# Norm steps and weight splits around five norms: their order on VectorE, ScalarE, GpSimd and TensorE

## The reference, cut to what matters

```python
def rms_norm(x, g):
    xf = x.astype(jnp.float32)
    y = xf * lax.rsqrt(jnp.mean(xf * xf, axis=-1, keepdims=True) + EPS)
    return (y * g.astype(jnp.float32)).astype(x.dtype)

def layer_norm(x, g, b):
    mu = xf.mean(-1, keepdims=True)
    var = jnp.square(xf - mu).mean(-1, keepdims=True)
    return ((xf - mu) * lax.rsqrt(var + LN_EPS) * g + b).astype(x.dtype)
...
        x = x + merged @ w_out[l]
        h2 = rms_norm(x, norm2[l])
        x = x + jnp.square(jax.nn.relu(h2 @ w_up[l])) @ w_down[l]
    return rms_norm(x, final_norm)
...
        x = layer_norm(DN_ALPHA * x + h, ln_g[i, 0], ln_b[i, 0])
        x = layer_norm(DN_ALPHA * x + swiglu_ffn(x, ffn_w_gate_up[i], ffn_w_down[i]), ln_g[i, 1], ln_b[i, 1])
```

## Time and profile before

| | |
|---|---|
| device time, median of 3 runs | 2143.26 us (2142.16 to 2143.68) |
| span of the profiled execution, first to last instruction | 2140.8 us, 2.5 below the median of the runs |
| TensorE, matmuls | busy 2097.3 us, 98% of the span |
| VectorE | busy 1180.6 us, 55% |
| ScalarE | busy 899.8 us, 42% |
| GpSimd | busy 504.1 us, 24% |
| granted TensorE clock, mean | 0.997 |

### The profile page before, as it was taken

The page is one execution under the profiler, slowest core; times in us unless marked ns, Lnnn a source line. Parts: engine busy times, 40 slices in busy tenths (PEclk is TensorE's granted clock), DMA queues, the critical chain, the costliest instruction groups (busy, mean ns, idle before and its releaser), DMA issues. The chain is left out here.

```text
span 2140.8 us, 34365 instructions
## 1 busy us (share of the span) xinstructions
PE 2097.3 (98%) x13883; PEld 1757.1 (82%) x13883; DVE 1180.6 (55%) x2031; ACT 899.8 (42%) x1574; POOL 504.1 (24%) x488
## 2 busy tenths in 40 slices
PE   8999999999999999999999999999999999999998
PEld 7877678988888897867878899899876678899887
DVE  5244546454343455557667678485555646576335
ACT  5454562333232335235444245243566634344231
POOL 4000000100000010211337456382432118363000
PEclk9999999999999999999999999999999999999999
DMA  5312233233333323210023323334342113334321
GB/s 170 98 50 69 60 88 100 70 109 99 98 95 92 99 83 87 79 32 2 3 63 85 112 82 100 99 99 118 79 100 65 51 51 93 94 95 143 99 89 60
DMA packets 341530, 179.64 MB, mean 84 GB/s; under 512 B 44342, under 2 KB 332260, under 8 KB 341372
## 3 DMA queue, kind: packets, MB, share of 16 engines
q1 hardware_dynamic: 339052, 171.54, 28.6%
q0 software_dynamic: 2320, 5.89, 1.0%
HBM read 172.40 MB, written 2.11 MB: 82 GB/s over the span
## 5 line engine op out<-in xcount | busy, mean ns | idle before, releaser
L602 PE MATMUL bank<-act_hi,w_hi 128*128 128x512 f32 (+1 forms) x1568 | 580.5, 370 | 9.5 <-DVE act_lo L1375 2.4
L585 DVE TENSOR_TENSOR w_lo<-w,w_hi 128x1024 fp32r<-128x1024 f32 (+2 forms) x314 | 406.0, 1295 | 317.7 <-ACT w_hi L577 317.3
L604 PE MATMUL bank<-act_hi,w_lo 128*128 128x512 f32 (+1 forms) x1568 | 560.7, 358 | 0.0
L603 PE MATMUL bank<-act_lo,w_hi 128*128 128x512 f32 (+1 forms) x1568 | 560.2, 357 | 0.0
L577 ACT ACTIVATE w_hi<-w 128x1024 fp32r<-128x1024 f32 (+2 forms) x315 | 316.6, 1013 | 294.1 <-PE bank L604 258.8
L602 PEld LDWEIGHTS bank<-act_hi,w_hi 128*128 128x128 f32 x1568 | 296.5, 189 | 63.6 <-issue 16.6
L604 PEld LDWEIGHTS bank<-act_hi,w_lo 128*128 128x128 f32 x1568 | 296.3, 189 | 44.4
L603 PEld LDWEIGHTS bank<-act_lo,w_hi 128*128 128x128 f32 x1568 | 297.0, 189 | 38.0 <-issue 0.7
L602 PE MATMUL bank<-hid_hi,w_hi 128*128 128x512 f32 (+1 forms) x672 | 248.5, 370 | 0.0
L604 PE MATMUL bank<-hid_hi,w_lo 128*128 128x512 f32 (+1 forms) x672 | 247.9, 369 | 0.0
L603 PE MATMUL bank<-hid_lo,w_hi 128*128 128x512 f32 (+1 forms) x672 | 247.9, 369 | 0.0
(11 more groups left out here) (543 smaller groups left out, 3537.3 us busy)
## 6 DMA issues: line engine op xcount, KB each, us to landing
w<-in_ffn_w_gate_up SPq DMA_DIRECT2D x76, 512.0 KB, 3.9
w<-in_w_in SPq DMA_DIRECT2D x41, 512.0 KB, 3.9
w<-in_w_up SPq DMA_DIRECT2D x32, 512.0 KB, 4.1
w<-in_w_down SPq DMA_DIRECT2D x32, 512.0 KB, 3.8
w<-in_ffn_w_down SPq DMA_DIRECT2D x32, 512.0 KB, 4.1
w<-in_even_w_in SPq DMA_DIRECT2D x28, 512.0 KB, 3.8
w<-in_ffn_w_down SPq DMA_DIRECT2D x16, 384.0 KB, 3.5
seven_w<-in_ffn_w_gate_up SPq DMA_DIRECT2D x24, 256.0 KB, 3.2
```

Source lines behind the costliest of these rows:

```text
L585: last = e.tensor_tensor(w_lo[:, at], src, w_hi[:, at].bitcast(F32), ALU.subtract)
L602: e.matmul(s.acc, *first, start=(k == 0), stop=False)
L603: e.matmul(s.acc, *second, start=False, stop=False)
L604: last = e.matmul(s.acc, *third, start=False, stop=(k == kt - 1))
```

## The change

Four things change, in the order of the title. `norms_first` names steps after which a norm's hooks come ahead of the weight split on ScalarE and VectorE, instead of behind it: T5 and T6 at the RMS edges, T6 at the LayerNorm edges. The first half's scaling of an RMS norm moves from T6 (tiles 0 to 3) and T7 (tiles 4 to 7) to T5 and T6. The first spread of a LayerNorm stands at the start of T7 (`a + 4.0`) instead of a quarter into it (`a + 4.25`). The low part of the last tile, `k` = 7, is made by VectorE instead of GpSimd in both halves of all five norms (`pool_lows`). What is computed stays the same.

```diff
         self.late = range(0)
...
@@ Gemm.run, scalar (and the same for vector)
                 s.job.epilogue.scalar(e, self, s)
+                if s.n in self.norms_first:
+                    for hook in hooks:
+                        hook.scalar_after(e, s.n)
                 for part in self.freed_at_once(s.n):
                     self.split_high(e, part)
-                for hook in hooks:
-                    hook.scalar_after(e, s.n)
+                if s.n not in self.norms_first:
+                    for hook in hooks:
+                        hook.scalar_after(e, s.n)
...
@@ Norm.__init__
-        split, odd = high is not None, n // 2
...
+        split = high is not None
+        self.pool_lows = tuple(range(1, min(n, KD - 1), 2))
+        self.dve_lows = tuple(k for k in range(n) if k not in self.pool_lows)
...
@@ Norm.vector_after
-                        if k >= first + 2 and k % 2 == 0 and self.high is not None:
+                        if k >= first + 2 and k - 2 in self.dve_lows and self.high is not None:
                             self.part_low(e, h, k - 2, self.lo)
...
@@ Norm.gpsimd
-            for k in range(1, self.n if self.high is not None else 0, 2):
+            for k in self.pool_lows if self.high is not None else ():
                 self.part_low(e, h, k, self.lo_pool)
...
@@ LayerNorm.gpsimd
-                for n, k in enumerate((1, 3, 5, 7, 0, 2, 4, 6)):
+                for n, k in enumerate(self.pool_lows + self.dve_lows):
...
@@ rms_between
+    g.norms_first |= {b - 2, b - 1}
     return Norm(core, lambda k: core.x[:, k, :], KD, squares, level=(a, b), root=(a + 2.75, head + 3.25),
-                scale=([(b - 1, 0, 4), (b, 4, KD)], b), **kinds)
+                scale=([(b - 2, 0, 4), (b - 1, 4, KD)], b), **kinds)
@@ ln_between
+    g.norms_first.add(b - 1)
     return LayerNorm(core, squares=squares, mean=(a + 1.5, head + 0.5), centre=(a, b), level=(a + 1, b),
-                     root=(a + 4.25, head + 3.25), scale=([(b - 1, 0, 4), (b, 4, KD)], b), **kinds)
+                     root=(a + 4.0, head + 3.25), scale=([(b - 1, 0, 4), (b, 4, KD)], b), **kinds)
```

More of the change, by code:

```diff
@@ L440, in __init__ @@
         self.SLOTS = slots
-        self.late = range(0)
+        self.late, self.norms_first = range(0), set()
         on_boundary(core, ctx, "w_gap", 512)
@@ L694, in _ @@
                 s.job.epilogue.vector(e, self, s)
+                if s.n in self.norms_first:
+                    for hook in hooks:
+                        hook.vector_after(e, s.n)
                 for part in self.freed_at_once(s.n):
                     self.split_low(e, part)
-                for hook in hooks:
-                    hook.vector_after(e, s.n)
+                if s.n not in self.norms_first:
+                    for hook in hooks:
+                        hook.vector_after(e, s.n)
             for hook in hooks:
@@ L1264, in __init__ @@
         self.scaled = Span(core.sig("norm_scaled"), H * n)
-        split, odd = high is not None, n // 2
-        self.hi, self.lo = Span(core.sig("norm_hi"), split * H * n), Span(core.sig("norm_lo"), split * H * (n - odd))
-        self.lo_pool = Span(core.sig("norm_lo_pool"), split * H * odd)
+        split = high is not None
+        self.pool_lows = tuple(range(1, min(n, KD - 1), 2))
+        self.dve_lows = tuple(k for k in range(n) if k not in self.pool_lows)
+        self.hi, self.lo = Span(core.sig("norm_hi"), split * H * n), Span(core.sig("norm_lo"), split * H * len(self.dve_lows))
+        self.lo_pool = Span(core.sig("norm_lo_pool"), split * H * len(self.pool_lows))
         place = 0
@@ L1307, in lo_at @@
     def lo_at(self, h, k):
-        i = (h * self.n + k) // 2 + 1
-        return self.lo_pool.at(i) if k % 2 else self.lo.at(i)
+        if k in self.pool_lows:
+            return self.lo_pool.at(h * len(self.pool_lows) + self.pool_lows.index(k) + 1)
+        return self.lo.at(h * len(self.dve_lows) + self.dve_lows.index(k) + 1)
     def take_sum(self, e, q):
@@ L1462, in gpsimd @@
             for h in range(2):
-                for n, k in enumerate((1, 3, 5, 7, 0, 2, 4, 6)):
+                for n, k in enumerate(self.pool_lows + self.dve_lows):
                     x = self.src(k)[:, HALVES[h]]
-                    e.wait_ge(*(self.hi if k % 2 else self.lo).at(h * self.n + k + 1 if k % 2 else h * EDGE + k // 2 + 1))
+                    e.wait_ge(*(self.hi.at(h * self.n + k + 1) if k in self.pool_lows else self.lo_at(h, k)))
                     e.tensor_scalar(x, x, self.b[:, k:k + 1], None, ALU.add).then_inc(self.placed.sem, 1)
-                    if k % 2:
+                    if k in self.pool_lows:
                         e.wait_ge(*self.placed.at(h * self.n + n + 1))
```

## The result

The changed kernel takes 2152.38 us (median of 4 runs, 2151.26 to 2154.12), the kernel before beside it 2142.91: +9.5 us, a ratio of 1.0039 (95% interval 1.0027 to 1.0052). It is slower, as forecast, and inside the stated range: 1.6 us above the forecast of 2150.8 and 0.2 above the rival with two clock drops, 2152.2. The profiled execution took 2154.12 us, 1.7 above that median. In the changed kernel lines 577 to 604 keep their numbers and the norms' are 11 higher (L1370 is now L1381, L1375 L1386, L1483 L1494, L1511 L1522, L1326 L1337); other variants shift them a little.

A forecast was written before the change was run, and what follows sets the result against it. TensorE, busy 98% of the span, was taken as the bound. RMS waits +3.9, LayerNorm edges +2.2 and clock +1.4 sum to +7.5 on 2143.3, forecasting 2150.8 us, range 2146.4 to 2153.4.

The forecast's parts named there:

- the rival with two clock drops: Both RMS waits lower TensorE's clock: 3.9 + 2.2 + 2.8, giving 2152.2 us; chance 0.27.
- RMS edges, the waits: At both RMS heads TensorE waits 3.3 us for the fourth tile's weights; 1.95 us later each, +3.9 us together.
- faster, as the edits aim: Rival: head tile 3's weights come in time although queued last; 3.9 us won, 2139.4 us; chance 0.07.
- TensorE's clock: Behind the two RMS waits the clock drops to 1.2 GHz, likeliest after one of them: +1.4 us.
- LayerNorm edges: At `up00`, `kv` and `up10` the second half's sums come later: 1.0 + 0.9 + 0.9 - 0.6 = +2.2 us.
- GpSimd's waits: In the LayerNorm edges' second half, TensorE's 0.2 us waits for tile 7's GpSimd low part go: -0.6 us.

The follow-up runs named there:

- the RMS part: Only the RMS-edge changes (T5 and T6 norms ahead of weight splits, first half scaled a tile sooner) against the kernel before: 2150.9 against 2143.56 us, +7.3.
- the order run: At RMS edges T6's norm ahead of its weight split, scaling passes left behind T6 and T7, against the kernel before: 2143.39 against 2143.3 us.
- LayerNorm order: Only T6's norm ahead of its weight split at LayerNorm edges, with the sooner spread, against the kernel before: 2144.54 against 2143.56 us, +1.0.

## Why the prediction was right, and which term was mis-sized

- **RMS edges, the waits: right to 0.04 us.** Foretold: first pass at 404.3, tile 2's low part done at 408.9, second pass at 409.2, tile 3 on TensorE at 413.95. Measured: 404.29, 408.94 (407.71 + 1.23), 409.18, 413.97. The rival "faster, as the edits aim" fell on the point that was given for it: the low part ended at 413.8, not by 410.5. That the place of T6's split is the cause is shown by undoing it alone (-3.0 us in place of +7.3).
- **TensorE's clock: the mis-sized term.** The step was "about two in three on each: one of the two is the likeliest, +1.4 us". It does not follow from its own chance: at two in three on each, two drops are as likely as one (0.44), and the mean is 1.9 us. Six waits of 3.2 us in three profiled executions (two of the changed kernel, one of the RMS part) were followed by a lower clock, six times of six, and the share was 2.9 and 4.1 us in the two of the changed kernel, 3.7 in that of the RMS part (its sums at 779.62) and 2.7 between its medians. The price of one drop was right where the clock was low for 3.4 us (1.3 to 1.6 us in three of the four of the changed kernel); in the fourth it was low for 6.8 and cost 2.7. My evidence was one stretch of 2.0 us with a drop and one of 1.6 without; a wait beyond both should have been taken as a drop each. The kernel before had one more stretch that I left out, a wait of 2.0 us with a drop (see the end). With two drops the working gives 2152.2, 0.2 below the median, or +8.9 where the kernel beside it gives +9.5. The Trainium skill (TensorE: Matmul & The Clock Gate, "Why this matters for your kernels") warns of long idle gaps between bursts, since one brings the clock back to half; the trace agrees, with a drop at each wait of 3.2 us and none at those of 1.2 us in the order run. The wait of 2.0 us with a drop is shorter than the gaps that it warns of; there the measurement decides.
- **LayerNorm edges: right within 0.3 us each.** Foretold +0.5 at the fourth tile and +0.9 up to the sums at `kv`; measured 0.5 and 1.15. Ahead of `up00` the foretold +1.0 came: the head starts 8.55 us later than before (1155.53 against 1146.98), the sums 9.52 (1164.72 against 1155.20). The collision of tile 7's low part with GpSimd's was the larger share and is shown by the run that moved it alone. The Trainium skill's rule (SBUF — State Buffer, "SBUF: two separate sides") lets the later of the two instructions wait for the whole of the earlier. The trace agrees in the main: 0.93 us for a low part that takes 0.47 alone, but it ended 0.29 after GpSimd's and not a full 0.47.
- **GpSimd's waits: right in sign, wrong in reading.** I took the three listed waits of 0.2 us for tile 7's. They are still there, three times 0.2: they are tile 5's. Tile 7's stood in no line of that view, and yet its end gave 0.33, 0.28 and 0.33 us, 0.9 in all and not 0.6. A matmul is shown 0.28 long while the next one starts after 0.12, so a hold of up to 0.16 is no idle time, and a longer one is listed short by as much. With the 1.15 in place of 0.9 at `kv` and the like at `up10`, the LayerNorm edges come to 2.4 us in the trace, near the foretold 2.2 because the two errors cancel.
- **The rest** of the profiled +11.6, some 1 us, is at places that the change does not touch (0.5 at `up00`'s mean, 0.6 in the attention behind `kv`); of those in the attention other profiles have some of either sign; the first comes again in most of the other runs (0.5 with tile 7's low part alone, none with the RMS part alone), never as a gain, and what brings it is not shown.

By parts: RMS +7.3, tile 7 +1.6, LayerNorm order +1.0, together 9.9, where the whole measured 9.5 and 9.9. Each part has an interval of some 2 us or more to either side, so that they add up so closely is partly luck.

## What to carry to other kernels

When an activation is made sooner at a hand-over between two products, list everything that the first k-step there needs, and find what the moved work now stands in front of: here 4.8 us won on one operand were lost on the weights of the fourth tile, and one split put back ahead of the second pass turned a loss of 7 us into a gain of 3. Where two engines make an operand in turn, only one of them may need the new order: with ScalarE left to split first, the LayerNorm order that cost 0.5 to 0.6 us at each of two edges won 0.65 there, in the traces. And a low part, or any small piece, that is moved to another engine should be judged per half, since the same move cost 1 us where that engine had urgent work behind it and won 0.3 where it had none.

## What was not expected of the hardware

- The same wait of 3.2 us at the same place cost 1.3 to 2.7 us in lower clock from one execution to the next: the sums behind the first RMS head stood 3.2 us later than before in one profile of the changed kernel (418.54) and 4.7 in the other (420.00), of which the wait is 1.95. The stretch at 0.50 lasted about twice as long in the second, and no run shows why.
- A wait of 1.2 us at the same tile was followed by no such drop, in the run of the order without the sooner scaling.
- Filling a wait with matmuls whose results nobody reads won 3.2 us over the two edges (778.75 against 775.52; 0.3 of it is a lead that this execution had before them) and cost nothing there; the medians show 1.3 to 2.7 of it, with intervals as wide as that.
- The trace of the kernel before, too, has a drop beside a shorter wait, and the prediction left it out. TensorE waits 1.97 us for `rw_M` up to 961.34, with the clock at 1.00, and goes on with small matmuls (64x64):

```profile
961.50:964.80 3.30, 3.15 (x46) 0.50 0.00 0
```

All fourteen profiled executions of this document have such a drop, at most 2.4 us behind the end of this wait; that the wait is its cause was not tested. The stretch of the earlier trace rows that the prediction went by, at 1709, has its drop in nine of the fourteen.
